# Small identity products on TensorE during the routing step, sample rows of the output projection in four column groups, and one wait taken out ahead of the extra loop

## The reference, cut to what matters

```python
u = h @ w_in                                   # one projection: q, k, v, z, xBC, dt, two gates
A = sliding_window_attention(q, k, v)
B = gated_rmsnorm(ssd(conv(xBC), dt), z)
mix = (sigmoid(gate_attn) * A + sigmoid(gate_ssd) * B) @ w_o
h = layer_norm(ALPHA * h + mix)
group = argmax(h @ rg_w + rg_b)                # 4 groups
top2  = top_k(expert logits inside the group)  # 8 experts of each group, 32 in all
y = sum over the two experts of p * (silu(h @ w_gate[e]) * (h @ w_up[e])) @ w_down[e]
h = layer_norm(ALPHA * h + y)
```

## Time and profile before

| what | us |
|---|---|
| median of three runs | 975.12 |
| the three runs | 979.6, 975.02, 975.12 |
| the profiled execution, its own time | 979.53 |
| its span (first to last instruction) | 977.8 |
| mean granted clock of TensorE, share of full | 0.921 |
| TensorE busy | 835.7 (85%) |
| VectorE busy | 473.9 (48%) |
| ScalarE busy | 261.9 (27%) |
| GpSimd busy | 199.3 (20%) |
| moved by DMA | 182.14 MB, mean 186 GB/s |

### The profile page before, as it was taken

How to read it: one execution, slowest core, us unless ns; L and a number is a source line. 1 busy time by engine, 2 the same in 40 slices (tenths; PEclk the granted TensorE clock), 3 DMA queues, 4 the chain that set the end, 5 groups by cost and what they waited for, 6 DMA issues and landing times.

```text
span 977.8 us, 12187 instructions
## 1 busy us (share of the span) xinstructions
PE 835.7 (85%) x4657; PEld 591.9 (61%) x4657; DVE 473.9 (48%) x1073; ACT 261.9 (27%) x647; POOL 199.3 (20%) x172
## 2 busy tenths in 40 slices
PE   5999798999989896999999899959999887756910
PEld 5997788989878895788888534557333332212300
DVE  5997376656565668793335223471121111101158
ACT  4221453434363247664320110110111110001100
POOL 2774534342013351110000000004111111011000
PEclk9999899999978797999999999969999998978965
DMA  8221211210061122752622490265999999997052
GB/s 306 86 88 29 69 54 35 65 35 32 1 253 54 43 93 108 267 180 117 259 87 86 182 419 2 94 254 218 358 429 421 425 422 424 422 426 308 32 186 86
DMA packets 34474, 182.14 MB, mean 186 GB/s; under 512 B 10997, under 2 KB 11653, under 8 KB 23858
## 3 DMA queue, kind: packets, MB, share of 16 engines
q1 hardware_dynamic: 25488, 159.24, 41.6%
q0 software_dynamic: 7744, 17.86, 5.2%
q10 hardware_dynamic: 1184, 4.26, 1.1%
HBM read 169.03 MB, written 20.77 MB: 194 GB/s over the span
## 4 chain that ended last, share of the span: by engine, by line
PE 64%; DVE 17%; DMA 12%; issue 3%; ACT 1%; SPq 1%; POOL 0%; POOLq 0%; DVEq 0%; ACTq 0%
PE bank L582 9%; PE bank L989 9%; PE bank L583 9%; PE bank L584 9%; DMA x_f<-in_w_gu 8%; PE bank L575 8%; DVE r_f L1445 5%; PE bank L998 4%; PE bank L974 2%; PE bank L766 2%; PE bank L672 2%; PE bank L706 1%; PE bank L798 1%; DMA x_f<-in_conv_state 1%; DMA small_f<-scr_h,x_f 1%
## 5 line engine op out<-in xcount | busy, mean ns | idle before, releaser
L989 PE MATMUL bank<-x_f,r_f 128*64 128x512 f32 x272 | 127.3, 624 | 19.7 <-ACT r_f L1369 11.1
L582 PE MATMUL bank<-r_r,w_r 128*128 128x268 f32 x416 | 126.0, 303 | 10.9 <-DVE w_r L1422 10.3
L583 PE MATMUL bank<-y_r,w_r 128*128 128x268 f32 x416 | 122.7, 295 | 0.0
L584 PE MATMUL bank<-r_r,w_r 128*128 128x268 f32 x416 | 122.5, 295 | 0.0
L583 PE MATMUL bank<-w_r,r_r 128*128 128x512 f32 x240 | 95.8, 399 | 0.0
L582 PEld LDWEIGHTS bank<-r_r,w_r 128*128 128x128 f32 x416 | 82.4, 198 | 15.8 <-DVE w_r L1422 10.3
L582 PE MATMUL bank<-x_r,r_r 128*128 128x512 f32 x200 | 81.5, 408 | 3.8 <-DVE w_r L1729 3.8
L989 PEld LDWEIGHTS bank<-x_f,r_f 128*64 128x64 f32 x272 | 38.4, 144 | 73.5 <-issue 72.5
L583 PEld LDWEIGHTS bank<-y_r,w_r 128*128 128x128 f32 x416 | 82.3, 198 | 0.0
L584 PEld LDWEIGHTS bank<-r_r,w_r 128*128 128x128 f32 x416 | 82.2, 198 | 0.0
L584 PE MATMUL bank<-x_r,w_r 128*128 128x512 f32 x200 | 80.0, 400 | 0.0
(11 more groups left out here) (359 smaller groups left out, 1562.4 us busy)
## 6 DMA issues: line engine op xcount, KB each, us to landing
x_f<-in_w_gu SPq DMA_DIRECT2D x17, 2048.0 KB, 27.6
w_f<-in_w_d SPq DMA_DIRECT2D x22, 1024.0 KB, 31.9
y_f<-in_w_gu SPq DMA_DIRECT2D x10, 2048.0 KB, 30.5
w_f<-in_w_f SPq DMA_DIRECT2D x26, 512.0 KB, 3.7
w_f<-in_w_gu SPq DMA_DIRECT2D x6, 2048.0 KB, 25.0
x_f<-in_w_d SPq DMA_DIRECT2D x11, 1024.0 KB, 31.4
w_f<-in_w_t SPq DMA_DIRECT2D x5, 2048.0 KB, 8.0
y_f<-in_state POOLq DMA_DIRECT2D x8, 512.0 KB, 5.1
```

Of the source, the lines that this page charges most:

```text
L582: pe.matmul(out, ah, bh, start=start, stop=False)
L583: pe.matmul(out, ah, bl, start=False, stop=False)
L584: return pe.matmul(out, al, bh, start=False, stop=stop)
L989: ins = pe.matmul(out[half, :], XT[:, k, half], wgu[s][:, k, :], start=(k == 0), stop=(k == KC - 1))
```

## The change

Three edits. First, the product of the 8 sample rows with `w_o` is cut in four along the contraction: each of the two column halves gets eight products as before, but product k writes to rows 32 j to 32 j + 31 of the bank, with j = k % 4, from a 32-column stationary tile (the 24 columns beyond the sample rows are set to zero by ScalarE). ScalarE then copies the four partial sums (`gpart`), and a product with a 0/1 matrix `gsum` adds them up. Second, TensorE runs 48 and then 32 products of the bfloat16 identity with itself, into a bank that nobody reads, ahead of the ranks and ahead of `pick_x(0)`. Third, the wait at L1388 is gone.

```diff
+N_BUSY = (48, 32)
+        gsum, gpart = cut(C1 + D, NSAMP), cut(C1, D)
...
+            def sample_parts():
+                pe.wait_ge(S["mt_ev"], 1)
+                for n in range(2):
+                    for k in range(KC):
+                        j = k % 4
+                        ins = pe.matmul(pb[2 + n][SROW * j:SROW * (j + 1), :], mT[0][:, k, 0:SROW],
+                                        (wo_a if k < KC // 2 else wo_b)[:, k % (KC // 2), n * 512:(n + 1) * 512],
+                                        start=(k < 4), stop=(k >= 4))
+                ins.then_inc(S["sp_mm"], 1)
+
+            def sample_sum():
+                pe.wait_ge(S["sp_ac"], 1)
+                for n in range(2):
+                    ins = pe.matmul(pb[2 + n][0:NSAMP, :], gsum, gpart[:, 512 * n:512 * (n + 1)], start=True, stop=True)
+                ins.then_inc(S["w_mm"], 1)
...
             turn_merged(0)
             turn_merged(1)
-            mix(0)
+            sample_parts()
             turn_merged(2)
+            sample_sum()
             mix(1)
...
+        def keep_busy(pe, n):
+
+            pe.wait_ge(S["lg_dv"], NT)
+            for _ in range(n):
+                pe.matmul(pb[7][:, 0:P], identb, identb, start=True, stop=True)
+
         def pe_rank(pe):
 
             pe.matmul(pb[5][:, 0:P], onesf, upper, start=True, stop=True).then_inc(S["rk_mm"], 1)
+            keep_busy(pe, N_BUSY[0])
             pe.wait_ge(S["rt_dv"], 2)
...
                 for t in range(NT):
                     r = tile_rows(t)
+                    if b == t == 0:
+                        keep_busy(pe, N_BUSY[1])
                     pe.wait_ge(S["hot_dv"], t + 1)
...
             def merged(t):
-                if t >= 2:
+                if t == 0:
+                    act.wait_ge(S["wr_in"], 16)
+                    act.activation(mT[0][:, :, NSAMP:SROW], wr[:, :, 0:SROW - NSAMP], ACT.Copy, scale=0.0)
+                if t == 2:
+                    act.wait_ge(S["sp_mm"], 1)
+                    act.copy(gpart[:, 0:512], pb[2][:, :])
+                    act.copy(gpart[:, 512:1024], pb[3][:, :]).then_inc(S["sp_ac"], 1)
+                if t > 2:
                     act.wait_ge(S["w_mm"], t - 1)
...
             before = 16 * len(range(1, FIRST, 2))
-            act.wait_ge(S["yw_out0"], 16 * len(range(0, FIRST, 2)))
             with act.Fori(0, extras) as j:
...
         def dve_gates(v):
+            v.tensor_reduce(gsum, ident.rearrange("p (j c) -> p c j", j=4)[:, 0:NSAMP, :], AX, ALU.add)
```

More of the change, by code:

```diff
@@ L328, in build @@
                      "sa_dv sa_mm sa_ac "
-                     "wt_in0 wt_in1 ln_in ln2_in xt_in wo_in c_mm c_ac c_dv kx_pl xr_in rms_ac mt_mm mt_ev w_mm lnb_dv lg_mm lg_dv rms_dv lv_dv lv_ac "
+                     "wt_in0 wt_in1 ln_in ln2_in xt_in wo_in c_mm c_ac c_dv kx_pl xr_in rms_ac mt_mm mt_ev sp_mm sp_ac w_mm lnb_dv lg_mm lg_dv rms_dv lv_dv lv_ac "
                      "none_pl id_out hot_dv rt_dv rt_ac rk_mm h1_out tb_in "
```

## The result

The changed kernel takes 961.31 us (median; 960.92 to 964.37), the kernel before beside it 975.07 (974.77 to 979.6): a ratio of 0.9865, 95% interval 0.9843 to 0.9887. The forecast was 960.8. The profiled execution took 960.92 us with a span of 959.1, against 979.5 and 977.8 before; the mean granted clock went from 0.921 to 0.930.

A forecast was written before the change was run, and what follows sets the result against it. It took TensorE (64% of the chain) as the bound, then the weight stream from about 696 to 890 us. Terms 8.4 + 1.0 + 4.9 = 14.3 off the median 975.1 gave 960.8 us (chance 0.50), range 955 to 967.

The forecast's parts named there:

- The sum: Whole kernel: gains of 8.4, 1.0 and 4.9 add to 14.3 us, taking the median from 975.1 to 960.8.
- The sample rows, 8.4: Output projection: a stretch of 15.5 us becomes 7.1 with four column quarters, a gain of 8.4 us.
- the clock at the start of the quarters: Sample-row products: 0.45 us added to 3.43 because the clock is still at half at their start.
- the forecast's own signs: Output projection: 32 instructions within 4 us, and the first 128-row `mix` 7.1 us after the turn of tile 1.
- The small products, 1.0: Route: identity products fit TensorE's idle time but longer pauses lose the clock; gain 1.0 us, bounds -1 to 4.6.
- the first rival: Route: small products hold the full clock, pick 9.3 us, gain 4.6 instead of 1.0, total 957.2 us; chance 0.28.
- The wait, 4.9: Extra loop: ScalarE copies 10.3 us earlier, but GpSimd's second table read limits the gain to 4.9 us; bounds 0 to 11.
- The late gather: Third pair's rows: a faster pick may delay their gather by 1 or 2 us, which the weight stream takes up.
- The quarters in turn: Rival, sample rows: the quarters do not overlap, so 8.4 becomes a loss of 2.1, total 971.3 us; chance 0.07.
- The wait was not hidden: Answers a rival, extra loop: the wait only moves to weights or table reads, 4.9 lost, 965.7 us; chance 0.09.
- The small products do not hold up the route: Answers a rival, route: products at whole latency, 0.46 us each, delay it 26 us, total 987.8 us; chance 0.03.
- The forecast's own sign of failure: Start of the experts: the prediction called itself wrong if they start less than 8 us earlier.

The follow-up runs named there:

- the repeat: The changed kernel run once more without an edit, in a later group: 963.16 us, ratio 0.9876 to the kernel before.
- the one-quarter kernel: The changed kernel with all eight products of each half written to the same 32 rows, only those copied and summed: 972.11 us, ratio 0.9956.
- the small products alone: The kernel before with only the 48 and 32 identity products added: 975.19 us, ratio 0.9982.
- reads together: The changed kernel with GpSimd's two table reads of the extra pass issued at once, ahead of the gather: 962.52 us, ratio 0.9858.
- read ahead: The changed kernel with the extra pass's first table column read one step ahead, the second at the head of the loop: 958.66 us, ratio 0.9825.
- the quarters in turn: The changed kernel with products dealt to quarters as k // 2 instead of k % 4, neighbours in the program sharing a quarter: 963.94 us, ratio 0.9887.
- the wait alone: The kernel before with only ScalarE's wait ahead of the extra loop taken out: 971.42 us, ratio 0.996.
- more small products: The changed kernel with 96 and 64 identity products instead of 48 and 32: 963.67 us, ratio 0.9871.
- the pick's new order: The changed kernel with 96 and 64 identity products and the 8-row tile last in the pick: 960.85 us, ratio 0.9842.
- the sample rows alone: The changed kernel with ScalarE's wait put back and no identity products: 969.44 us, ratio 0.9923.
- all but the small products: The changed kernel with no identity products (counts 0 and 0): 965.18 us, ratio 0.9879.

## Why the prediction was right

**The sum.** 14.3 us were forecast; the medians give 13.8, the ratio 13.2, and the repeat's ratio 12.1. The two large terms came out by their mechanisms, each a little under its forecast by ratio (7.5 for 8.4, 3.9 for 4.9). That the medians agree to 0.5 us is in part luck.

**The sample rows, 8.4.** The trace gives 7.8, the ratio of this part alone 7.5. The zero fill was costed at 0.33 and took 0.36, the sum at 1.72 and took 1.88, the gap for the copies at 0.1 and was 0.18. The step that was mis-sized is the clock at the start of the quarters: 0.45 us was allowed for it, since the old product had paid 0.74. But the clock stayed at half until 555.5, four of the eight rounds, and that cost 1.7; hence 5.25 and not 3.9. So two of the forecast's own signs failed: the 32 instructions were not done within 4 us, and tile 1 began 8.3 us after its turn and not 7.1. What made up for most of it was not in the sum: the clock now fell behind the turn of tile 1 and not ahead of it, so that this turn took 1.07 in place of 1.94. That is luck. The overlap itself, read from four products in the earlier trace rows, held, and the one-quarter kernel shows that without it there is no gain.

**The small products, 1.0.** Inside the bounds of -1 to 4.6, but no run shows the term: by ratio it is 1.8 alone and 0.3 to 1.4 on top of the rest, all within the noise. The pick itself was 2.9 shorter, and 11.0 lies below the 12 to 14 that the forecast named as its sign. The argument had two halves. That a better clock makes longer pauses, and that these cost the pick its clock, fits the profiles: where the first 48 met a full clock they took 2.85 us and left 3.3, and the pick took 12.6 to 12.9 (the small products alone, reads together, read ahead); where they met half a clock they filled the pause, and it took 11.0 (the changed kernel twice, the quarters in turn, one quarter). The small products have the shortest pick where the clock is worst when the route begins. The other half was missing: with no pause left, the clock still fell, and not with the 8-row tile last. I had listed a pick of 9.3 as the first rival, tied to pauses alone; it took 96 and 64 products and another order to get it. The step that does not hold is that an earlier end of the pick moves the experts microsecond for microsecond. The kernels with a pick of 11.0 reach the extra rows 202.6 to 203.0 us after its start, those with 12.9 (reads together, read ahead) in 202.7 and 202.8: the late gather of the third pair stands in the first and not in the second.

**The wait, 4.9.** Measured 4.9 in the profile and 3.9 by ratio. Every step of the chain came out: ScalarE copies at once, GpSimd asks for the second column right behind the gather, and that column releases the scatter. The two experiments on the table reads bear it out: with the reads together the first gather is held and nothing is gained; with the first read taken off the chain it is 3.9 or 5.0 us more by the ratios.

**The late gather.** Forecast as a delay of 1 or 2 us that the stream takes up, with its cause: loads asked for earlier lie beside GpSimd's table writes, as the 6.60 us show. TensorE waited 2.71 us, and the down products behind it took 4.43 us in the chain at a fallen clock; together the third pair's loads lost 4 us (13.8 to 9.8 early). By the turn of the extra rows, after thirteen pairs, the lead was 14.1 again. The delay was larger than forecast. It was made up on the way, but so was the gain of the pick, as said above, and how much of each the stream took up stays open.

**The rivals.** The quarters in turn cost 9 to 11 us in a kernel that really works in turn (all in one quarter), close to the 10.5 that separated that rival from the forecast. The wait was not hidden. The small products do not hold up the route: 32 at half clock took 3.41 us, 0.107 each, and the pick began 11.9 us after the product ahead of the first of them (630.56), as it did before (641.27, 12.0). The forecast's own sign of failure, experts less than 8 us earlier, did not come: they were 13.8 earlier, 10.7 without the 3.1 that arose before 553.5.

What stays open is the 2 to 4 us in which equal kernels differ. From the start of the pick to the turn of the extra rows it takes 202 to 203 us in most profiles (the changed kernel twice, the wait alone, reads together, read ahead, more small products, the two kernels on the quarters), 201.7 with the pick's new order, and 205 to 206 in the others (before, the sample rows alone, the small products alone, all but the small products). The clock falls in waits for weights on the way, but I found no edit that selects one or the other.

## What to carry to other kernels

Where an output has few rows, split the products over the array's column quarters and sum the parts: it is the overlap that pays, so look in the profile for any such product and read its time in fours. Small products in TensorE's idle time can raise the clock and shorten what follows; those sized for the half clock left pauses at the full one, and in this kernel it took the order with the 8-row tile last to keep the clock. But look first at what the next stage waits for: here the shorter pick brought nothing in the whole time that is clear of noise. Before a wait is taken out, follow the queue that it released to its next wait; what is found there is the gain, and the next thing to move.

## What was not expected of the hardware

- Products that fill only 8 rows of the array were followed by a fall of the granted clock 1.8 us into a stretch of unbroken work (646.6, after a pause of 0.33); the same products at the end of the pick were not, and 64 instructions on 128 rows ran at 1.00. Eight rows do not do it alone: the second pick begins with them and keeps the full clock (64 instructions in 7.60 us).
- Products of identity, whose result nobody reads, were followed by a rise of the clock from 0.50 (631.0 to 634.0) to full; without them it stayed at 0.50 from 632 to 652.
- Products for different column quarters run at once even where neighbours in the program share a quarter: those of `w_f` started 0.03 us after those of `x_f`, four of whose products stand ahead of them. Whether the engine or the build of the program put them so, the trace does not say. The Trainium skill, "TensorE: Matmul & The Clock Gate", in its Part 3 on packing small matmuls, says that matmuls start and end in program order; if the program kept the order in which it was written, these rows speak against it.
- A read of 0.2 KB took 8 to 10 us under the full weight stream; two asked for together took 9.2 us each (median from issue to landing).
